# Two attention stages with key blocks handled two at a time: half as many, twice as wide copies of the transposed probabilities, and two score banks where there were three

## The reference, cut to what matters

```python
def mla_attention(q, k, v):                 # 8 heads, 2048 queries, 2048 keys
    ...
        sc = jnp.einsum('bqhd,bkhd->bhqk', qb, k).astype(jnp.float32) * scale
        causal = key_pos[None, :] <= qpos[:, None]
        sc = jnp.where(causal[None, None], sc, -jnp.inf)
        p = jax.nn.softmax(sc, axis=-1).astype(v.dtype)
        return jnp.einsum('bhqk,bkhd->bqhd', p, v)

def dsa_attention(q, k, v, q_idx, k_idx, w_idx, k_top):   # 8 heads on 2 key heads, selected keys
    ...
        sc = jnp.einsum('bqkgd,bqjkd->bqkgj', qg, kg).astype(jnp.float32) * scale
        sc = jnp.where(valid[:, :, None, None, :], sc, -jnp.inf)
        p = jax.nn.softmax(sc, axis=-1).astype(v.dtype)
        o = jnp.einsum('bqkgj,bqjkd->bqkgd', p, vg)
```

## Time and profile before

| | |
|---|---|
| median of 3 runs | 3423.64 us (3419.33 to 3426.46) |
| profiled execution, its own time | 3424.3 us |
| its span in the trace | 3422.5 us |
| stage MLA in the trace | about 446 to 938 us |
| stage DSA in the trace | about 1613 to 2077 us |
| busy share of the span | PE 93%, PEld 78%, DVE 61%, ACT 53%, POOL 23% |
| mean granted TensorE clock | 0.964 of full speed |

### The profile page before, as it was taken

The page is one execution under the profiler, slowest core; times in us unless marked ns, Lnnn a source line. Parts: engine busy times, 40 slices in busy tenths (PEclk is TensorE's granted clock), DMA queues, the critical chain, the costliest instruction groups (busy, mean ns, idle before and its releaser), DMA issues. The chain is left out here.

```text
span 3422.5 us, 51529 instructions
## 1 busy us (share of the span) xinstructions
PE 3171.4 (93%) x17464; PEld 2665.5 (78%) x17464; DVE 2079.6 (61%) x5117; ACT 1820.8 (53%) x3608; POOL 775.1 (23%) x1078
## 2 busy tenths in 40 slices
PE   7999879999989999996899995999989999969998
PEld 5888668888768777775677775999878888869997
DVE  5766768888746756653899885434446666632112
ACT  5565557777656666653777773111246666632121
POOL 5444401011101112231211001100034444311110
PEclk9999989999999999998999997999999999969999
DMA  5666654336152222225211104544441221144332
GB/s 170 201 205 195 198 131 107 76 69 141 58 202 81 71 82 80 81 86 127 60 40 42 31 7 152 172 147 134 145 136 55 73 73 53 55 136 138 123 124 74
DMA packets 307189, 370.47 MB, mean 108 GB/s; under 512 B 24800, under 2 KB 251936, under 8 KB 303088
## 3 DMA queue, kind: packets, MB, share of 16 engines
q1 hardware_dynamic: 293728, 320.77, 32.4%
q0 software_dynamic: 13200, 46.42, 4.2%
HBM read 216.32 MB, written 150.80 MB: 107 GB/s over the span
## 5 line engine op out<-in xcount | busy, mean ns | idle before, releaser
L93 PE MATMUL i_p_g<-i_hT_lo,i_wh 128*128 128x512 f32 x768 | 308.5, 402 | 9.3 <-DVE i_wl L1632 9.3
L94 PE MATMUL i_p_g<-i_hT_hi,i_wl 128*128 128x512 f32 x768 | 306.6, 399 | 0.0
L95 PE MATMUL i_p_g<-i_hT_hi,i_wh 128*128 128x512 f32 x768 | 306.5, 399 | 0.0
L1650 DVE SCALAR_TENSOR_TENSOR i_score<-i_relu,i_w,i_score 128x1024 f32<-128x1024 f32 (+7 forms) x154 | 155.1, 1024 | 168.4 <-ACT i_relu L1534 166.5
L1544 ACT ACTIVATE i_above<-i_score,i_less 128x2048 bf16<-128x2048 f32 (+13 forms) x140 | 183.2, 1308 | 106.6 <-POOL i_less L1601 69.6
L1081 DVE TENSOR_TENSOR mla_tl<-mla_p_t,mla_th 128x512 fp32r<-128x512 f32 (+1 forms) x320 | 186.1, 606 | 45.3 <-ACT mla_th L1124 41.6
L1124 ACT ACTIVATE mla_th<-mla_p_t 128x512 fp32r<-128x512 f32 (+1 forms) x320 | 163.9, 530 | 86.3 <-PE mla_p_t L1021 83.6
L1081 DVE TENSOR_TENSOR dsa_tl<-dsa_p_t,dsa_th 128x512 fp32r<-128x512 f32 x272 | 179.9, 686 | 39.8 <-ACT dsa_th L1124 33.7
L1051 DVE CUSTOM_DVE_ANT_0 dsa_probs<-dsa_p_s,dsa_mask 128x512 f32<-128x512 f32 (+3 forms) x320 | 184.6, 605 | 25.4 <-PE dsa_p_s L1790 23.8
L1124 ACT ACTIVATE dsa_th<-dsa_p_t 128x512 fp32r<-128x512 f32 x272 | 155.2, 593 | 67.3 <-PE dsa_p_t L1021 66.4
L1021 PE MATMUL mla_p_t<-ident,mla_probs 128*128 128x128 f32 x1088 | 172.7, 274 | 11.1 <-DVE mla_tl L1081 9.7
(11 more groups left out here) (340 smaller groups left out, 9768.8 us busy)
## 6 DMA issues: line engine op xcount, KB each, us to landing
scratch_gates<-i_ob SPq DMA_DIRECT2D x96, 256.0 KB, 2.4
m_m<-scratch_gates SPq DMA_DIRECT2D x64, 256.0 KB, 4.6
f_hs<-scratch_h2T SPq DMA_DIRECT2D x16, 1024.0 KB, 10.0
scratch_qkT<-b_th SPq DMA_DIRECT2D x64, 192.0 KB, 2.5
scratch_qkT<-b_tl SPq DMA_DIRECT2D x64, 192.0 KB, 2.9
i_ws<-in_w_in SPq DMA_DIRECT2D x24, 512.0 KB, 4.5
b_xt<-in_x SPq DMA_DIRECT2D x16, 512.0 KB, 4.8
scratch_h<-b_xh POOLq DMA_DIRECT2D x16, 512.0 KB, 3.0
```

The lines of the kernel that those rows point to most:

```text
L93: pe.matmul(out, l[0], r[1], start=start, stop=False)
L94: pe.matmul(out, l[1], r[0], start=False, stop=False)
L95: return pe.matmul(out, l[0], r[0], start=False, stop=stop)
L1650: nc.vector.scalar_tensor_tensor(out=acc, in0=r, scalar=w[:, t, h:h + 1], in1=acc, op0=ALU.mult, op1=ALU.add).then_inc(summed, 1)
```

## The change

Whole key blocks are taken two at a time (`block_pairs`; an odd one and the narrow ones of the diagonal stay alone). Eight transposes fill two neighbouring banks, and one ScalarE copy and one VectorE subtraction each go over both banks. `p_s` has 2 banks, `p_t` 2 pairs of banks. M is one block step behind its T and issues the two hi matmuls first, waits for lo, and then the two lo matmuls. `th` and `tl` have 3 places of two blocks in DSA, 2 in MLA.

```diff
...
-    split_ring = 4
-    lag = 3
-    score_banks = 3
+    split_ring = 3
+    lag = 1
+    score_banks = 2
...
+def block_pairs(blocks):
+
+
+    whole = [b for b in blocks if not b[1]]
+    return [whole[i:i + 2] for i in range(0, len(whole), 2)] + [[b] for b in blocks if b[1]]
...
-        b_steps = [("B", m, i, j, s0) for i, (j, s0) in enumerate(units[m]["blocks"])] + [("V", m)] if m >= 0 else []
+        b_steps = [("B", m, i, part) for i, part in enumerate(block_pairs(units[m]["blocks"]))] + [("V", m)] \
+            if m >= 0 else []
...
-            blocks += steps[-1][0] == "B"
+            if steps[-1][0] == "B":
+                blocks += len(steps[-1][3])
...
-    n_b = [sum(len(u["blocks"]) for u in units[:n]) for n in range(len(units) + 1)]
+    n_p = [sum(len(block_pairs(u["blocks"])) for u in units[:n]) for n in range(len(units) + 1)]
     A = layer.score_banks
-    B = 6 - A
-    ring = lambda n, place: (n_b[n] + n + place) % B
+    B = (6 - A) // 2
+    ring = lambda n, place: (n_p[n] + n + place) % B
...
-        th = sb("th", [P, S, GT], F32R)
-        tl = sb("tl", [P, S, GT], F32R)
+        th = sb("th", [P, S, 2, GT], F32R)
+        tl = sb("tl", [P, S, 2, GT], F32R)
...
-        p_t = c.enter_context(nc.psum_tensor(f"{tag}_p_t", [P, B, GT], F32))
+        p_t = c.enter_context(nc.psum_tensor(f"{tag}_p_t", [P, B, 2, GT], F32))
...
             def multiply():
-                n, place, j, s0 = behind.pop(0)
-                b = n_b[n] + place
+                n, place, part = behind.pop(0)
+                b, first = n_p[n] + place, part[0][1]
                 if place == 0:
                     layer.wait_values(pe, n)
                     if n >= 2:
                         pe.wait_ge(output_read, n - 1)
+                out = p_o[:, n % 2, first * P:GT]
+                ends = place == n_p[n + 1] - n_p[n] - 1
                 pe.wait_ge(hi_done, b + 1)
-                out = p_o[:, n % 2, s0 * P:GT]
-                v, last = layer.values(n, j), place == len(units[n]["blocks"]) - 1
-                hi, lo = th[:, b % S, s0 * P:GT], tl[:, b % S, s0 * P:GT]
-                if layer.packed:
-                    nc.tensor.matmul(out, v, hi, start=place == 0, stop=False)
-                    pe.wait_ge(lo_done, b + 1)
-                    nc.tensor.matmul(out, v, lo, start=False, stop=last).then_inc(multiplied, 1)
-                else:
-                    nc.tensor.matmul(out[0:HD], v[:, 0:HD], hi, start=place == 0, stop=False)
-                    nc.tensor.matmul(out[0:HD], v[:, HD:P], hi, start=False, stop=False)
-                    pe.wait_ge(lo_done, b + 1)
-                    nc.tensor.matmul(out[0:HD], v[:, 0:HD], lo, start=False, stop=last)\
-                        .then_inc(multiplied, 1)
+                for y, (j, _) in enumerate(part):
+                    nc.tensor.matmul(out, layer.values(n, j), th[:, b % S, y, first * P:GT],
+                                     start=place + y == 0, stop=False)
+                pe.wait_ge(lo_done, b + 1)
+                for y, (j, _) in enumerate(part):
+                    last = nc.tensor.matmul(out, layer.values(n, j), tl[:, b % S, y, first * P:GT],
+                                            start=False, stop=ends and y == len(part) - 1)
+                last.then_inc(multiplied, 1)
...
-                    for s in range(s0, 4):
-                        last = nc.tensor.transpose(p_t[:, ring(n, place), s * P:(s + 1) * P],
-                                                   probs[n % R][:, s, j * P:(j + 1) * P], ident[:])
+                    for y, (j, first) in enumerate(part):
+                        for s in range(first, 4):
+                            last = nc.tensor.transpose(p_t[:, ring(n, place), y, s * P:(s + 1) * P],
+                                                       probs[n % R][:, s, j * P:(j + 1) * P], ident[:])
                     last.then_inc(turned, 1)
-                    behind.append((n, place, j, s0))
+                    behind.append((n, place, part))
                     if len(behind) > layer.lag:
                         multiply()
...
-                    nc.vector.tensor_tensor(tl[:, b % S, s0 * P:GT], p_t[:, ring(n, place), s0 * P:GT],
-                                            th[:, b % S, s0 * P:GT].bitcast(F32),
+                    nc.vector.tensor_tensor(tl[:, b % S, 0:len(part), at], p_t[:, ring(n, place), 0:len(part), at],
+                                            th[:, b % S, 0:len(part), at].bitcast(F32),
                                             ALU.subtract).then_inc(lo_done, 1)
...
-                    nc.scalar.activation(th[:, b % S, s0 * P:GT], p_t[:, ring(n, place), s0 * P:GT],
+                    nc.scalar.activation(th[:, b % S, 0:len(part), at], p_t[:, ring(n, place), 0:len(part), at],
                                          ACT.Copy).then_inc(hi_done, 1)
...
     tag = "mla"
+    split_ring = 2
...
```

More of the change, by code:

```diff
@@ L979, in multiply @@
                         pe.wait_ge(output_read, n - 1)
+                out = p_o[:, n % 2, first * P:GT]
+                ends = place == n_p[n + 1] - n_p[n] - 1
                 pe.wait_ge(hi_done, b + 1)
[L981 to L993 removed]
+                for y, (j, _) in enumerate(part):
[6 more added lines that the diff above has]
+                last.then_inc(multiplied, 1)
             def wait_bank(n, place):
[L997 removed]
+                r = n_p[n] + n + place - B
                 if r < 0:
                     return
[L1000 to L1001 removed]
+                m = max(x for x in range(n + 1) if n_p[x] + x <= r)
+                if r - n_p[m] - m == n_p[m + 1] - n_p[m]:
                     pe.wait_ge(spread_done, m + 1)
@@ L1015, in _ @@
                 elif step[0] == "B":
-                    _, n, place, j, s0 = step
+                    _, n, place, part = step
                     if place == 0:
@@ L1028, in _ @@
                     n = step[1]
-                    place = len(units[n]["blocks"])
+                    place = n_p[n + 1] - n_p[n]
                     wait_bank(n, place)
@@ L1032, in _ @@
                     for s in range(4):
-                        last = nc.tensor.transpose(p_t[:, ring(n, place), s * P:(s + 1) * P],
+                        last = nc.tensor.transpose(p_t[:, ring(n, place), 0, s * P:(s + 1) * P],
                                                    inv[:, n % 2, s:s + 1].broadcast_to([P, P]), ident[:])
@@ L1048, in _ @@
                         if n >= R and s == 0:
-                            dve.wait_ge(turned, n_b[n - R + 1])
+                            dve.wait_ge(turned, n_p[n - R + 1])
                     dve.wait_ge(scored, i + 1)
@@ L1075, in _ @@
                 elif step[0] == "B":
-                    _, n, place, j, s0 = step
-                    b = n_b[n] + place
+                    _, n, place, part = step
+                    b, at = n_p[n] + place, slice(part[0][1] * P, GT)
                     if b >= S:
@@ L1091, in _ @@
                     n = step[1]
-                    dve.wait_ge(multiplied, n_b[n + 1])
+                    dve.wait_ge(multiplied, n_p[n + 1])
                     dve.wait_ge(spread_done, n + 1)
@@ L1130, in _ @@
                         act.wait_ge(output_read, n - 1)
-                    nc.scalar.activation(spread[:, n % 2], p_t[:, ring(n, len(units[n]["blocks"]))],
+                    nc.scalar.activation(spread[:, n % 2], p_t[:, ring(n, n_p[n + 1] - n_p[n]), 0],
                                          ACT.Copy).then_inc(spread_done, 1)
@@ L1201, in sync_unit @@
         if n == NG * (H - 1):
-            sp.wait_ge(self.sems["multiplied"], self.sems["n_b"][n])
+            sp.wait_ge(self.sems["multiplied"], self.sems["n_p"][n])
             self.index_in.load_h(sp, 0)
@@ L1222, in load_unit @@
         if h >= 2 and g == 0:
-            sp.wait_ge(self.sems["multiplied"], self.sems["n_b"][NG * (h - 1)])
+            sp.wait_ge(self.sems["multiplied"], self.sems["n_p"][NG * (h - 1)])
         for half in range(2):
```

2 lines of the change are left out of this document (1 added, 1 removed).

## The result

| | before | changed |
|---|---|---|
| median | 3424.69 us | 3578.73 us (3573.58 to 3580.22, 4 runs) |
| profiled execution, span | 3422.5 us | 3576.1 us |
| mean granted TensorE clock | 0.964 | 0.962 |

The ratio is 1.045, 95% interval [1.0437, 1.0464]: 154 us slower. The forecast was slower, 3518 us with a range of 3450 to 3575; the time lies above the range, and the loss is 1.6 times the forecast 94 us.

The account below looks back on a forecast made before the run. Leads were taken to hang on VectorE's passes, block steps on TensorE. The terms 66 + 9 + 11 + 10 + 23 - 25 = 94 us on 3424.3 gave 3518 us, range 3450 to 3575.

Parts of the forecast that it names:

- What the change saves: Copies and subtractions: wider ones save 12 us on engines that idle there, covered by TensorE in block steps; taken as 0.
- A: Leads of both stages: with two score banks a bank's round trip is no longer hidden, +66 us.
- B: End of a DSA unit: the last pair's subtraction ends later, so the next lead's passes start later, +9 us.
- F: Block steps: two thirds of today's 37 us of `p_t` waits fall away, -25 us.
- C: Pairs with no score step between: M's lo matmuls wait for lo, 0.17 us per pair, +11 us.
- D: MLA's narrow blocks with nothing between: each takes a whole pair place, M one step behind, +10 us.
- E: Block steps with one score step: a row's Exp ahead of a copy makes lo late, +23 us.
- slower by more: One pair behind is too short, steps near an Exp or O stall: +160 us and more, 3585; chance 0.12.

Follow-up runs that it names:

- d_single: The changed kernel with pairs copied and subtracted one block at a time; 3542.42 us, ratio 1.0348.
- f_early: d_single with the first block's copy allowed to start after its own four transposes; 3519.59 us, ratio 1.0281.
- a_banks: The kernel before with 2 score banks in place of 3 and four single `p_t` banks, nothing paired; 3470.14 us, ratio 1.0139.
- h_early_lag2: f_early with M two pairs behind its T in DSA; 3516.99 us, ratio 1.0263.
- c_lag2: The changed kernel with M two pairs behind its T in DSA alone; 3559.36 us, ratio 1.0405.
- b_lag: The kernel before with M one block behind its T in place of three; 3617.43 us, ratio 1.0567.

## Why the prediction was wrong, by its own steps

- **What the change saves (0 taken): no saving shows.** d_single and f_early are 36 and 59 us faster than the changed kernel with 448 instructions more, so the width costs more than the instructions save; what these save by themselves was not measured. The Trainium skill, Perfetto Trace Analysis, section "Optimizing Scalar/DVE Operations", says that where ScalarE and VectorE are not saturated but cause bubbles on other engines, breaking up instructions may let work be completed sooner. These two runs agree with it. The same section's rule on larger operations is given for a saturated engine; VectorE was busy 404 of 464 us in DSA before the change, and merging brought no gain there.
- **A (66 us): right; B (9 us): about half.** The leads took 71 us more, 66 of them in a_banks too; what is left for B is 5 us in DSA. MLA g = 2 went from 5.20 to 6.40 us (forecast +1.2), g = 3 from 4.99 to 6.52 (+1.6), g = 1 from 5.27 to 6.83 (+1.7); only g = 0 was smaller, 2.06 to 2.35 and not +0.7. a_banks shows the cause of A; no run changed B alone.
- **F (-25): right.** a_banks' block steps have 21 us less.
- **C, D and E (11 + 10 + 23 = 44 us): the step that failed.** Against a_banks the changed kernel's block steps take 62 + 34 = 96 us more. The mechanism was right, M's lo matmuls wait for a late subtraction; the sum was less than half of what was measured. Two things were missing. First, the restart: each wait costs TensorE about 0.11 us more than its length (0.57 and 0.46 above). In the PE timeline the start behind a waiting lo group comes that much later than its columns need in 176 places, 19 us. The prediction had no such term.

  Second, C and D counted too few waits, and took each as if ACT and DVE had nothing else to do. I read the distance from the hi to the lo matmuls of each M in the trace and took off what it is without a wait. Pairs with no score step between lose 27 us where C had 11. There are 79 of them, and C counted 64: the others stand in MLA units whose few score steps do not reach between all pairs. 55 with no Exp near lose 0.25 us each where C had 0.17, and 24 with one lose 0.5 (E had given Exps to steps with a score step alone). MLA's blocks that stand alone with no score step between lose 17 us where D had 10. The steps of E proper lose 22, as forecast.

  27 + 17 + 22 + 19 is 85 of the 96. M's hi matmuls wait for copies in 17 places in MLA, 5.7 us; the rest is open. (The 109 us of waits in the PEld rows are not the loss: lo came 66 us late in sum.)

One of the narrow ones, on PE (a block of 384 columns, in the unit shown above):

```profile
...
727.18 0.38 PE L1028 MATMUL mla_p_t<-ident,mla_probs 128*128 128x128 f32 x2
727.45 0.44 PE L993 MATMUL mla_p_o<-mla_th,mla_v 128*128 128x384 f32 x1
728.12 0.44 PE L997 MATMUL mla_p_o<-mla_tl,mla_v 128*128 128x384 f32 x1 [0.23 <-DVE mla_tl L1088]
728.39 0.27 PE L1028 MATMUL mla_p_t<-ident,mla_probs 128*128 128x128 f32 x1
...
```

From hi to lo are 0.67 us where 384 columns took 0.26 in the kernel before (769.00 to 769.26 us of its PE timeline), and the next T follows 0.27 us after, where it was 0.17.

- **By cause, from the runs.** Of the 96 us, the width of copy and subtraction is 31 (changed to d_single), the late signal for the first block 19 (d_single to f_early), and 8 in DSA the distance from T to M (f_early to h_early_lag2). These shares hold in this order only, since each remedy shortens the same waits: the distance taken first is worth 25 us in DSA (c_lag2). The other 39 are left in MLA, where the space for a third place of `th` and `tl` was lacking and M's distance was not changed in any pair kernel. The trace shows where they stand. In the 14 MLA units with no score step between the blocks, the block steps take 79 us in a_banks and 102 in f_early; from the first narrow block on to V it is 27.5 and 43.4 us, and this end of the unit took 41.4 in the changed kernel, so neither single nor early copies helped it. That it is so long because each narrow block has a pair's place to itself and M is one narrow step behind is argued, not shown.
- **The range** reached to 3575. The bounds for C, D and E were 90 us in all; what was measured for them, 96, lies above those bounds, which left out the restart. The case "slower by more" (chance 0.12, 3585) came near in its time, but not in its make-up: it had A at 80 and E at 50 us where 66 and 22 were measured, so its number is luck. The prediction also gave only 0.06 to all times above 3575, half of what it gave to this one case, whose own time lies there.

## What to carry to other kernels

Where one engine's work hides a chain over two others, halving the number of that chain's instructions by doubling their width makes the chain longer (3.48 us from T to lo for a pair here, where the prediction worked out 2.1 for a single block), and the consumer pays for it if it stands only one step behind. Count banks by their round trip (producer's latency + reader + handover, here 1.64 and 1.87 us) against the slower engine's pace: in DSA three banks (0.55 us per chunk against VectorE's 0.61) hid it, two (0.82) did not, and that could be worked out ahead to within some us. A wait in the stream of matmuls costs its length and a restart, and the sum of the weight loads' waits is not the loss: it was 109 us in the changed kernel, where lateness and restarts make 85, and 172 in b_lag, whose block steps took 192 us more. Read the loss from distances between starts.

## What the runs showed of the hardware that was not expected

- After a wait, two 512 column matmuls take 0.57 us until the next instruction's start, and 0.46 without. The kernel before has it too: in the lead of DSA tile 8 the first of the two score matmuls behind the wait takes 0.34 us until the second starts (1760.81 to 1761.15), and 0.24 with no wait (1759.54 to 1759.78).

```profile
...
1759.54 0.39 PE L1789 MATMUL dsa_p_s<-dsa_k_hi,dsa_q 128*128 128x512 f32 x1
1759.78 0.40 PE L1790 MATMUL dsa_p_s<-dsa_k_lo,dsa_q 128*128 128x512 f32 x1
...
1761.15 0.39 PE L1790 MATMUL dsa_p_s<-dsa_k_lo,dsa_q 128*128 128x512 f32 x1
...
```

- The granted TensorE clock fell inside the stages of the changed kernel, where the kernel before had 1.00 throughout 640 to 930 us and 1650 to 2040 us: 0.66 in 710 to 720 us, 0.77 in 1755 to 1785 us (window rows above). 0.66 means that part of the stretch ran at the lower of its two levels, 1.2 GHz in place of 2.4; a 512 column matmul takes 0.43 us there (713.48 to 713.90) and 0.23 else. Two MLA leads of a class that takes 6.84 us elsewhere took 8.16 and 8.17, one of them there. Ahead of these stretches TensorE was busy 137.6 of 150 us (560 to 710) and 28.1 of 40 us (1715 to 1755). By such comparisons with like units this is, as an estimate, some 10 us of the 154, part of it in the leads; no run separated it. Pairs are not needed for it: a_banks has such stretches too (0.83 in 680 to 700 and 710 to 730 us, 0.80 in 1690 to 1715), so hardly any of the 96 us against a_banks is the clock. Nor do long waits of M alone bring it: b_lag, whose leads are those of the kernel before, has 1.00 in 470 to 1037 and 1745 to 2270 us. Of a_banks, then of b_lag (the same columns as in the window rows above):

```profile
...
680.00:700.00 20.00, 19.47 (x105) 16.14 (x104) 14.63 (x42) 12.30 (x26) 1.89 (x2) 0.83 0.17 43
710.00:730.00 20.00, 18.46 (x80) 14.17 (x79) 15.25 (x55) 10.42 (x21) 3.76 (x4) 0.83 0.61 112
...
1690.00:1715.00 25.00, 20.47 (x97) 16.85 (x97) 17.58 (x63) 13.89 (x28) 4.72 (x6) 0.80 0.28 58
...
```

```profile
...
470.00:1037.00 567.00, 515.18 (x2735) 389.08 (x2733) 412.39 (x1200) 331.24 (x583) 56.54 (x60) 1.00 0.33 75
1745.00:2270.00 525.00, 452.91 (x2305) 318.86 (x2306) 402.19 (x1129) 316.27 (x512) 56.51 (x60) 1.00 0.12 28
...
```
